# Four reorderings in one long fp32 layer kernel: last attention, chunk turns, cross-attention, memory

## The reference

```
def mem_cross_attn(h, mem, w_q, w_kv, w_o):          # 4 heads of 256
    q = heads(h @ w_q); k, v = split(mem @ w_kv)
    p = softmax(q @ k.T * 256**-0.5)                 # 512 x 256 for each head
    return merge(p @ v) @ w_o

# SSM: x, B and C are columns of one projection, through a 4 tap convolution and silu
z, xbc, dt = split(h @ w_in); xbc = silu(causal_dwconv(xbc, conv_w, conv_b))

# last attention, for each of 16 heads
o = g0 * softmax(q k_cmp) v_cmp + g1 * softmax(q_rot k_sel) v_sel + g2 * softmax(q_rot k_win) v_win
```

## Time and profile before

| | before |
|---|---|
| median of 3 runs | 2827.34 us (2823.39 to 2827.55) |
| profiled execution | 2827.59 us |
| its span, all instructions | 2825.9 us |
| mean granted TensorE clock | 0.966 |
| TensorE busy, instructions | 2597.7 us, 13316 |
| VectorE busy | 1353.7 us |
| ScalarE busy | 1072.6 us |
| GpSimd busy | 206.6 us |

### The profile page before, as it was taken

One profiled execution on the slowest core, in us unless ns is written; L12 is line 12 of the kernel. 1 busy time (PEld: TensorE's weight loads), 2 busy tenths in 40 slices (PEclk: granted clock), 3 DMA queues, 4 the chain that ended last, 5 costly groups with the idle time before them and its releaser, 6 DMA issues.

```text
span 2825.9 us, 35051 instructions
## 1 busy us (share of the span) xinstructions
PE 2597.7 (92%) x13316; PEld 2104.6 (74%) x13316; DVE 1353.7 (48%) x1870; ACT 1072.6 (38%) x1569; POOL 206.6 (7%) x249
## 2 busy tenths in 40 slices
PE   6978799799999988898899999999987888999999
PEld 5855588588887777685478888888875666888887
DVE  5764346378853354424644633244535444433323
ACT  2235432315452154335644333233424444433322
POOL 1101101010000000001201000010001111100000
PEclk9989999899999999999999999999979999999999
DMA  7730054235423222220013522223210000132222
GB/s 248 266 121 1 26 186 146 75 120 172 170 82 112 90 63 74 75 90 31 1 68 105 193 89 84 102 95 100 92 53 23 15 15 15 60 104 89 96 99 80
DMA packets 178692, 263.21 MB, mean 93 GB/s; under 512 B 8233, under 2 KB 127905, under 8 KB 178593
## 3 DMA queue, kind: packets, MB, share of 16 engines
q1 hardware_dynamic: 156608, 194.00, 20.9%
q0 software_dynamic: 15232, 58.72, 5.8%
q10 hardware_dynamic: 6752, 9.09, 1.0%
HBM read 255.51 MB, written 2.10 MB: 91 GB/s over the span
## 4 chain that ended last, share of the span: by engine, by line
PE 77%; DVE 10%; ACT 6%; issue 3%; POOL 3%; DMA 0%; ACTq 0%; DVEq 0%; SPq 0%; POOLq 0%
PE ps L689 21%; PE ps L691 20%; PE ps L690 20%; PE ps L1290 2%; PE ps L916 2%; ACT decay L1884 1%; DVE wlo L2096 1%; PE ps L958 1%; PE ps L1395 1%; ACT pnt_h L1995 1%; DVE pnt_l L2100 1%; PE ps L1210 1%; DVE nst L2635 1%; POOL diag L2896 1%; PE ps L1236 1%
## 5 line engine op out<-in xcount | busy, mean ns | idle before, releaser
L2096 DVE TENSOR_TENSOR wlo<-raw,whi 128x2048 fp32r<-128x2048 f32 x180 | 412.2, 2291 | 730.2 <-ACT whi L1515 730.2
L689 PE MATMUL ps<-acth,wlo 128*128 128x512 f32 (+1 forms) x1888 | 702.9, 372 | 24.5 <-DVE actl L2100 12.2
L691 PE MATMUL ps<-acth,whi 128*128 128x512 f32 (+1 forms) x1888 | 695.9, 369 | 0.0
L690 PE MATMUL ps<-actl,whi 128*128 128x512 f32 (+1 forms) x1888 | 695.8, 369 | 0.0
L1515 ACT ACTIVATE whi<-raw 128x2048 fp32r<-128x2048 f32 x180 | 343.7, 1910 | 571.5 <-PE ps L691 571.5
L689 PEld LDWEIGHTS ps<-acth,wlo 128*128 128x128 f32 x1888 | 357.9, 190 | 88.0 <-DVE actl L2100 14.7
L690 PEld LDWEIGHTS ps<-actl,whi 128*128 128x128 f32 x1888 | 357.8, 190 | 59.3 <-issue 1.2
L691 PEld LDWEIGHTS ps<-acth,whi 128*128 128x128 f32 x1888 | 357.4, 189 | 59.5
L689 PE MATMUL ps<-whi,hid_l 128*128 128x512 f32 x528 | 208.5, 395 | 5.2 <-DVE conv_t L2326 3.4
L690 PE MATMUL ps<-wlo,hid_h 128*128 128x512 f32 x528 | 206.8, 392 | 0.0
L691 PE MATMUL ps<-whi,hid_h 128*128 128x512 f32 x528 | 206.7, 391 | 0.0
(11 more groups left out here) (329 smaller groups left out, 3689.2 us busy)
## 6 DMA issues: line engine op xcount, KB each, us to landing
mraw<-in_mod_w POOLq DMA_DIRECT2D x48, 1024.0 KB, 5.5
raw<-in_ffn_w_in SPq DMA_DIRECT2D x44, 1024.0 KB, 4.9
raw<-in_ffn_up SPq DMA_DIRECT2D x22, 1024.0 KB, 4.9
raw<-in_ssm_w_in SPq DMA_DIRECT2D x20, 1024.0 KB, 5.0
raw<-in_ffn_w_out SPq DMA_DIRECT2D x20, 1024.0 KB, 5.0
raw<-in_sb_win SPq DMA_DIRECT2D x12, 1024.0 KB, 5.0
raw<-in_ffn_down SPq DMA_DIRECT2D x10, 1024.0 KB, 4.9
raw<-in_xa_wkv SPq DMA_DIRECT2D x8, 1024.0 KB, 5.0
```

Source lines behind the costliest of these rows:

```text
L689: nc.tensor.matmul(o, ll, rh, start=start, stop=False, skip_group_check=True)
L690: nc.tensor.matmul(o, lh, rl, start=False, stop=False, skip_group_check=True)
L691: return nc.tensor.matmul(o, lh, rh, start=False, stop=stop, skip_group_check=True)
L2096: nc.vector.tensor_tensor(wlo[:, slot, :], raw[:, slot, :], whi[:, slot, :].bitcast(F32), ALU.subtract) \
```

## The change

**Last attention.** TensorE no longer issues the outputs of job n - 1 in one piece. A round's strips are issued ahead of the same round of job n: strip 0, round 0, strips 1 and 3, round 1, strip 2, round 2. Each strip waits only for its own low part, and each round waits for the low part of the round that used its bank. VectorE makes the reciprocal and factor of job n ahead of all four maxima of job n + 1.

**Chunks.** `turn_chunks` moves from behind a pair to behind bank 0 of the next pair. The dt weights are split on ScalarE and VectorE two pairs earlier, and TensorE waits for the freed banks behind the dt product instead of ahead of it.

**Cross-attention.** The scores of head 0 go into the second query pair, behind its second bank, into banks 4 and 5; ScalarE's exponentials and VectorE's maxima and normalising of head 0 go there too. The rest is written out in a new order with two buffers for the turned probabilities. The output projection starts with the first four chunks, and waits for the other four at its second unit.

**Memory.** The DMA is issued in the seventh pair's turn of stick-breaking attention; TensorE turns the memory into banks 0 to 3 in the turn behind it, between the values of pair 6 and the first units of pair 7 (counted from 0), and ScalarE and VectorE split it there. The wait on `o_free` moves behind the memory's projections. GpSimd's next loads of modulation weights wait for the last pair's weights instead of for `o_free`.

The core of the diff (line numbers of its own file are left out; the same moves on ScalarE and VectorE are cut to the order of their calls):

```diff
 # tiles
-    meml = place("meml", [P, KC, MEM], F32R, at=o); o += 8192
+    meml = place("meml", [P, KC, MEM], F32R, at=ARENA + 49152)
-    pxt = place("pxt", [P, MB, SEQ], at=o); o += 4096
+    pxt = [place("pxt0", [P, MB, SEQ], at=o), place("pxt1", [P, MB, SEQ], at=ARENA)]; o += 4096
+    SCORE_BANK = (4, 2, 0, 2)
+    ROUND_STRIPS = ((0,), (1, 3), (2,))
...
 # tensor: memory
+            def memory_turned():
+                pe.wait_ge(mem_in, 16)
+                pe.wait_ge(sp_ready, 2 * KC)
+                for t in range(MB):
+                    for j in range(2):
+                        for c in range(4):
+                            last = nc.tensor.transpose(ps[:, 2 * t + j, P * c:P * c + P],
+                                                       mem_t[:, t, P * (4 * j + c):P * (4 * j + c) + P], ident[:])
+                        last.then_inc(turned, 1)
+                turns(turned_free, 2 * MB)
...
                     values(pair - 1)
+                if pair == KC - 1:
+                    memory_turned()
                 if pair < KC:
                     head_units(pair)
-            pe.wait_ge(o_free, 2 + KC)
-            turns(o_free, KC)
...
 # tensor: cross-attention
+            head_turn(0)
+            head_scores(1)
+            head_values(0)
+            head_scores(2)
+            head_turn(1)
+            head_scores(3)
+            head_turn(2)
+            head_values(1)
+            head_turn(3)
+            head_values(2)
+            head_values(3)
...
 # tensor: last attention
                     for r, blocks in enumerate(ROUNDS):
+                        if n:
+                            strip_outputs(n - 1, ROUND_STRIPS[r])
+                        if n == QG and r == 2:
+                            pair_outputs(0, g)
+                        if r == 0:
+                            pe.wait_ge(n_diag, turns(n_diag))
+                        if n or r == 2:
+                            round_taken(1)
...
 # tensor: program
-        pe.wait_ge(mem_in, 16)
-        to_features(mem_t, MB)
         turns_out()
         feature_pairs(2, memh, meml, MEM)
         token_pairs(2, memh, meml, nt=MB)
+        pe.wait_ge(o_free, 2 + KC)
+        turns(o_free, KC)
...
-        feature_pairs(1, acth, actl, mods=4)
+        banks_out()
+        feature_turn(acth, actl, behind={(0, 1): lambda: head_scores(0)})
+        mod_columns(4)
+        mods_behind[0] += 1
         cross_attention()
         banks_out()
-        token_product(acth, actl, KC, h_sum, summed, mods=4)
+        token_product(acth, actl, KC, h_sum, summed, mods=4,
+                      before_unit=lambda u: pe.wait_ge(heads_free, 4 * u + 4))
...
-        first_pair(h_sum, scaled, conv_done, after=turn_chunks)
-        feature_pairs(3, acth, actl, free=conv_done, after=turn_chunks, extra=tok_steps, out=False)
+        first_pair(h_sum, scaled, conv_done)
+        feature_pairs(3, acth, actl, free=conv_done, behind={(0, 0): turn_chunks}, extra=tok_steps, out=False)
+        feature_pairs(1, acth, actl, free=conv_done, behind={(0, 0): turn_chunks}, extra=tok_steps, out=False)
         feature_pairs(1, acth, actl, free=conv_done, out=False)
-        feature_pairs(1, acth, actl, free=conv_done)
...
 # scalar: cross-attention (query_pairs: exps(0) behind the first unit's split)
+            turned_probs(0)
+            exps(1)
+            high(0)
+            turned_probs(1)
+            exps(2)
+            exps(3)
+            turned_probs(2)
+            high(1)
+            turned_probs(3)
+            high(2)
+            high(3)
...
 # vector: last attention
-                    if n + 1 < 2 * QG:
-                        for tb in (3, 2, 0):
-                            maximum(n + 1, tb)
...
                     if n + 1 < 2 * QG:
-                        maximum(n + 1, 1)
+                        for tb in T_STRIPS:
+                            maximum(n + 1, tb)
```

More of the change, by code:

```diff
@@ L704, in turns_out, with feature_turn @@
             pe.wait_ge(turned_free, turns.seen.get("turned_free", 0) + 4)
-        def feature_turn(ah, al, n=SEQ, free=bank_free, behind={}):
+        def feature_turn(ah, al, n=SEQ, free=bank_free, behind=None):
             for u in range(2):
@@ L764, in first_turn, with first_pair @@
                             last.then_inc(marks, 1)
-        def first_pair(before, turn, free=bank_free, mods=0, after=None):
+        def first_pair(before, turn, free=bank_free, mods=0):
             first_turn(before, turn, lambda u: pe.wait_ge(free, turns(free)))
@@ new lines, in head_scores @@
+        def head_scores(hd):
+            if hd == 0:
+                pe.wait_ge(turned_free, turns.seen["turned_free"] + 4)
+            for t in range(TB):
+                bank = SCORE_BANK[hd] + t // 2
+                if t % 2 == 0:
+                    if hd == 1:
+                        pe.wait_ge(bank_free, turns.seen["bank_free"] + bank + 1)
+                    if hd == 3:
+                        pe.wait_ge(probs, 8)
+                for c in range(2):
+                    last = nc.tensor.matmul(ps[:, bank, MEM * (t % 2):MEM * (t % 2) + MEM],
+                                            qx[:, 2 * hd + c, P * t:P * t + P], kx[:, 2 * hd + c, :],
+                                            start=t % 2 == 0 and c == 0, stop=c == 1, skip_group_check=True)
+                if t % 2:
+                    last.then_inc(scores, 1)
@@ L1255, in job_outputs, with round_taken @@
                              n % 4 == 0 and sb == 0, False)
+            def round_taken(ahead):
+                pe.wait_ge(n_lo, turns.turn * 24 + turns.seen.get("n_lo", 0) + ahead)
             def pair_outputs(pair, g):
@@ L1664, in weights, with memory_high @@
                 last.then_inc(w_ready, 1)
+            def memory_high():
+                for r in range(2 * MB):
+                    t, j = divmod(r, 2)
+                    act.wait_ge(turned, turns(turned))
+                    nc.scalar.activation(memh[:, 4 * j:4 * j + 4, P * t:P * t + P], in_chunks(ps[:, r, :]), ACT.Copy) \
+                        .then_inc(turned_hi, 1)
+                turns(turned_free, 2 * MB)
             exponentials(0)
@@ L2260, in maxima, with memory_low @@
                                                    op1=ALU.max).then_inc(sp_ready, 1)
+            def memory_low():
+                for r in range(2 * MB):
+                    t, j = divmod(r, 2)
+                    block = (slice(None), slice(4 * j, 4 * j + 4), slice(P * t, P * t + P))
+                    dve.wait_ge(turned_hi, turns(turned_hi))
+                    lo_part(meml[block], in_chunks(ps[:, r, :]), memh[block]).then_inc(turned_free, 1)
             caps(0)
@@ new lines, in stick_breaking, with maxima @@
+                if pair == KC - 1:
+                    memory_low()
+        def maxima(hd):
+            b = 4 * (hd % 2)
+            for k in range(2):
+                dve.wait_ge(scores, 2 * hd + k + 1)
+                last = nc.vector.tensor_reduce(small[:, 16 + b + 2 * k:18 + b + 2 * k],
+                                               ps[:, SCORE_BANK[hd] + k, :].rearrange("p (t m) -> p t m", t=2),
+                                               AX.X, ALU.max)
+            last.then_inc(dve_step, 1)
+            dve.wait_ge(dve_step, turns(dve_step))
+            nc.vector.tensor_scalar(small[:, b:b + 4], small[:, 16 + b:20 + b], -1.0, None, ALU.mult) \
+                .then_inc(score_max, 1)
@@ L2303, in cross_attention, with query_splits, low @@
+        def query_splits():
+            mod_units(0, 2)
+            split(0)
+            maxima(0)
+            mod_units(2, 2)
+            normalise(0)
+            split(1)
+            turns(marks, 4)
+            mod_store(4, 56)
+        def cross_attention():
+            def low(hd):
                 for c in range(2):
@@ L2305, in cross_attention @@
                     lo_part(actl[:, 2 * hd + c, :], ps[:, 6 + c, :], acth[:, 2 * hd + c, :]).then_inc(heads_free, 1)
+            maxima(1)
+            normalise(1)
+            low(0)
+            maxima(2)
+            normalise(2)
+            maxima(3)
+            normalise(3)
+            low(1)
+            low(2)
+            low(3)
         def conv_ffn():
```

177 lines of the change are left out of this document (76 added, 101 removed).

## The result

| | before | after |
|---|---|---|
| median (lowest to highest), us | 2825.36 (2822.23 to 2827.55) | 2726.79 (2726.08 to 2731.55) |
| ratio, 95% interval | | 0.965 (0.9638 to 0.9663) |
| profiled execution / span, us | 2827.59 / 2825.9 | 2727.47 / 2725.8 |
| mean granted clock | 0.966 | 0.978 |

The changed kernel is 98.6 us faster, by medians; the two profiled executions are 100.1 apart.

What follows compares the result with a forecast made beforehand. TensorE itself was 77% of the chain of waits; only less waiting in its queue or a higher clock helps. Terms 12.9 + 25.4 + 21.2 + 11.9 + 20.7 = 92.1 gave 2735.5, taken as 2737 us; 8-in-10 range 2718 to 2765.

Steps and rivals of the forecast that it cites:

- memory: Turn from stick-breaking attention to the memory: 11.8 us of waiting goes, turning costs 1.0, clock gives 2.1; gain 12.9 us.
- cross-attention: Modulation columns to output projection: 59.7 us falls to 34.3 at full clock with 2 us of waits; gain 25.4 us.
- chunks: SSM projection's chunk turns: four visits cost 7.2 us instead of 29.8, with a weight unit 1.4 late; gain 21.2 us.
- dt product: The dt product follows the sixth pair directly at the full clock, without 9.70 us idle ahead; gain 11.9 us.
- last attention: Last attention: jobs fall from 6.99 to about 6.25 us apart, over 28 distances; gain 20.7 us.
- margin of -1.5: Whole kernel: 2735.5 us taken as 2737, since small new waits are likelier than small gifts.
- the ring named: Last attention: low part of round 2, factor, diagonal, rounds 0 and 1 with strips, round 2 again; 6.2 us a job.
- Rival one: The last attention gives nothing, as three queues are in its ring: 2758 us, chance 0.12.
- rival two: Packed stretches (cross-attention, chunks, memory, dt product) keep a low clock or get weight units late: 2757 us, chance 0.16.
- rival three: Last attention: interleaving makes each round wait a full trip through ScalarE and VectorE, jobs 11.4 us: 2880 us, chance 0.02.
- Rival four: Moved pieces hang on a late counter, so two still run at their old place: half the gain, 2782 us, chance 0.05.
- the trace agrees: Cross-attention: the trace fits the Trainium skill's rule that gaps between matmul bursts put the clock back to half rate.

Runs made afterwards that it cites:

- u3: The changed kernel with cross-attention in its old order on all engines, one buffer for the turned probabilities: 2752.27 us.
- x3: The changed kernel with head 0's scores behind the query pair's last bank, its exponentials, maxima and normalising behind the pair's splits: 2735.96 us.
- u2: The changed kernel with the chunk turns behind the pair again, the dt weights still early: 2750.06 us.
- u5: The changed kernel with the dt weights split at the old place and the wait for all banks ahead of the dt product again: 2740.70 us.
- x1: The changed kernel's last attention with VectorE's factor between the low parts of rounds 1 and 2, but TensorE's outputs in one piece: 2733.09 us.
- v1: The changed kernel with VectorE's old order in the last attention (three maxima ahead of the factor), TensorE's strips still dealt: 2764.23 us.
- w1: The changed kernel with VectorE's factor of the next job moved up again, between the low parts of rounds 1 and 2: 2714.59 us.
- x2: The changed kernel with the memory still loaded early, but turned and split only behind the last values of stick-breaking attention: 2726.37 us.

## Why the prediction was right

By the lengths of the same stages in the two traces (profiled executions; the stages are those of the table above):

| term | forecast | measured |
|---|---|---|
| memory | 12.9 | 12.9 |
| cross-attention | 25.4 | 27.8 |
| chunks | 21.2 | 20.9 |
| dt product | 11.9 | 11.9 |
| last attention | 20.7 | 23.3 |
| code outside | margin of -1.5 | 3.5 |

- **Memory.** The 11.8 us went whole, and the first product came 0.0 behind the last values. The turning cost 0.78, for 1.0 forecast; the clock was 1.00 as taken, and that gave 1.9 for 2.1.
- **Cross-attention.** The mechanism held, and the term of 2 us of waits left was too large: 0.9 was measured, at the turnings of heads 2 and 3. The whole stretch took 29.0 plus 3.45 for the scores of head 0, so 32.5 where 34.3 was forecast. The prediction had read the wait at the start as 2.3, and the row has 3.35; this is outside its sum. u3 took back 25.5 by medians and 27.1 in its stage. x3 shows that the place of head 0's scores, which the prediction priced as costing "the same 3.47 inside the pair as outside", is worth 6.5 by itself, because the softmax of head 0 needs that time.
- **Chunks.** The pairs are 23.5 apart for 23.6 forecast, without a wait at the transposes, and the first one has the late weight unit in it, at 1.9 for 1.4. All as worked out; u2 took back 23.3 (22.3 in its stage).
- **dt product.** Directly behind the pair, at the upper level. u5 took back 13.9 by medians, 11.8 in its stage.
- **Last attention.** The distance was forecast at 6.25 and is 6.25, on the ring named. That the term came within 2.6 is in part luck. The 28 distances were priced at 20.7 and gave 17.7, because two in each group are not steady ones: the job with the pair's output went from 8.2 to 7.9, and the last job of a group got longer, 5.7 to 6.2. The three steps from group to group, which the prediction let cancel, gave 5.8 (12.5 each, for 14.1 to 15.0 before). What lies ahead of the first diagonal gave 1.7, and what lies behind the last one cost 1.8. The prediction did not ask either what each half of the edit does alone. The square of runs does: the factor's move brings most, and dealing without it costs.
- **The margin.** The step that failed is the last one, "small new waits are likelier than small gifts". The code outside the five stages gave 3.5: -1.0 up to the seventh pair, +1.6 from the first feed-forward to the SSM projection, -0.7 from the scan on, +2.5 in the 80 us ahead of the last attention, +1.0 behind it. They follow no edit: the same stretch between the end of the scan's inputs and the last attention took 862.1 before, 860.2 after, and 858.1 to 865.3 in the undone kernels.

The +2.5 goes with the clock. The two windows end where the last attention begins and hold the same work but for one instruction, before and after (columns as above), in a stretch where TensorE stands idle often:

```profile
2110.00:2143.00 33.00, 23.14 (x55) 0.81 0.14 32
```

```profile
2037.00:2067.00 30.00, 20.07 (x54) 0.90 0.15 35
```

The 80 us (from the copy of the compressed keys, `kcmp`, to the first `pn`) took 82.2 before and in u2, u3, u5 and x3, and 79.6 to 79.9 after and in seven of the others; x1 had 81.1. So the same code has mainly two lengths, and nothing in the runs says which a kernel gets.

Rival one (attention gives nothing) fell to the 6.25; rival two to the clock of 1.00 in all windows; rival three to jobs of 6.25. Interleaving did lengthen the job in v1, to 7.50, but not by the trips that rival three feared: the wait there is for the diagonal. Rival four fell to the five undone parts.

## What to carry over

When work is dealt out to fill an engine's waits, first list every ring that closes over one round, with its length; moving filler into the longest ring makes it longer (v1), and it pays only when another edit has made that ring the shorter one. So try both edits and their square before crediting either. Put products that feed a chain of small steps on other engines (a softmax) inside the stretch before, not at its end: this saves the wait and the low clock behind it. And judge an edit of 3 us at its place in the trace, since unchanged code moves by as much.

## What the runs showed of the hardware

**The clock at the start differs between kernels with the same code there.** TensorE in the first 100 us of the kernel before, after, and of w1, with the early factor (the window's columns as above):

```profile
0.00:100.00 100.00, 78.19 (x353) 0.97 0.71 249
```

```profile
0.00:100.00 100.00, 77.53 (x347) 0.90 0.70 246
```

```profile
0.00:100.00 100.00, 77.52 (x352) 0.97 0.72 249
```

The DMA moves as much and TensorE is as busy, and the granted clock is 0.97 or 0.90. The last two kernels differ only in the last attention, 2000 us later, so the edit doesn't explain it. Over the other kernels it goes from 0.88 (x3) to 1.00 (v1), and the times do not follow it: the same high part around 161 us comes 0.8 earlier than after's in v1 and 1.8 earlier in x2, whose clock was 0.91. Each row is one profiled execution; what decides the clock there stays open.

**A wait of 2.19 us left the clock at its upper level, one of 4.52 did not** (x2 and x3), and behind the longer one it took 6.4 us of matmuls at 0.70 on average. The cost of the longer wait was 4.5 + 2.0. The length of a wait doesn't decide alone. In the kernel before, heads 1 and 2 of cross-attention have the same waits, 2.33 ahead of the turning and 0.74 ahead of the values, and the same eight value products take (chain of waits)

```profile
537.83 3.70 PE ps L1062 x8
...
549.14 5.41 PE ps L1062 x8
```

The granted clock was 1.00 in the first and 0.68 in the second, and in u3, with the same order of work, the two took 3.70 and 5.31 again. So the prediction's "the trace agrees" holds for the 3.35 ahead of the first scores, behind which the clock was 0.72, while shorter waits went both ways. What else decides it stays open.
